# The mLSTM layer's work placed between the units of its projections and its out-projection, in a four-stage decoder trunk on one core

## The reference, cut to what matters

```python
p = h @ w_in                      # q, k (512 each), v, o (1024 each), input and forget gates (4 each)
log_f = log_sigmoid(fg + b_f)     # b = cumsum(log_f) per head
m_t = maximum(b + m, max_s(b_t - b_s + i_s))
s_qk = (q @ k.T) * exp(dmat - m_t)          # causal
num = w_inter * (q @ C) + s_qk @ v
den = w_inter * (q @ n) + sum(s_qk)
h = num / maximum(abs(den), exp(-m_t))
C_new = decay * C + sum_s w_k[s] * k_s v_s^T     # n_new, m_new likewise
out = (head_rms(h, g_head) * sigmoid(o)) @ w_out
```

## Time and profile before

| | us |
|---|---|
| median of 3 runs | 2936.16 |
| lowest, highest | 2926.19, 2954.83 |
| the profiled execution | 2929.75 |
| its span, from the first to the last instruction | 2928.2 |
| PE busy | 2748.8 |
| DVE, ACT, POOL busy | 1316.7, 883.4, 188.5 |

### The profile page before, as it was taken

The page is one execution under the profiler, slowest core; times in us unless marked ns, Lnnn a source line. Parts: engine busy times, 40 slices in busy tenths (PEclk is TensorE's granted clock), DMA queues, the critical chain, the costliest instruction groups (busy, mean ns, idle before and its releaser), DMA issues.

```text
span 2928.2 us, 49999 instructions
## 1 busy us (share of the span) xinstructions
PE 2748.8 (94%) x21504; PEld 2635.3 (90%) x21504; DVE 1316.7 (45%) x2071; ACT 883.4 (30%) x1092; POOL 188.5 (6%) x164
## 2 busy tenths in 40 slices
PE   7999999776988999999999999999799889999998
PEld 7999999745987799999999999999796875999998
DVE  5444223315466344443344433667434563444422
ACT  4332221221323233322222222443322322333322
POOL 2000000001100010000000000001210100100000
PEclk9999999985899999999999999999888989999999
DMA  4333323103257132333233333223123382333331
GB/s 122 89 93 102 95 76 88 42 8 105 84 159 251 60 93 87 93 105 90 79 91 88 107 90 79 68 67 86 29 69 101 103 286 88 87 87 92 104 93 55
DMA packets 472038, 277.42 MB, mean 95 GB/s; under 512 B 24753, under 2 KB 460722, under 8 KB 471875
## 3 DMA queue, kind: packets, MB, share of 16 engines
q1 hardware_dynamic: 458662, 239.76, 28.6%
q0 software_dynamic: 8704, 33.56, 3.2%
q10 hardware_dynamic: 4552, 2.36, 0.3%
HBM read 258.16 MB, written 17.68 MB: 94 GB/s over the span
## 4 chain that ended last, share of the span: by engine, by line
PE 86%; DVE 6%; ACT 4%; issue 2%; DMA 1%; POOL 0%; ACTq 0%; SPq 0%; DVEq 0%; POOLq 0%
PE ACC L433 24%; PE ACC L435 23%; PE ACC L434 23%; PE ACC L1119 2%; PE M L1942 1%; ACT w_hi L516 1%; PE ACC L1942 1%; PE M L1419 1%; DVE w_lo L522 1%; PE M L1462 1%; DVE cache L1215 1%; PE M L2019 1%; PE M L2081 1%; PE M L1872 0%; PE ACC L1450 0%
## 5 line engine op out<-in xcount | busy, mean ns | idle before, releaser
L433 PE MATMUL ACC<-xg_hi,w_hi 128*128 128x260 f32 x3968 | 1127.6, 284 | 11.1 <-DVE w_lo L894 7.6
L435 PE MATMUL ACC<-xg_hi,w_lo 128*128 128x260 f32 x3968 | 1123.9, 283 | 0.0
L434 PE MATMUL ACC<-xg_lo,w_hi 128*128 128x260 f32 x3968 | 1120.2, 282 | 0.0
L522 DVE TENSOR_TENSOR w_lo<-raw,w_hi 128x1024 fp32r<-128x1024 f32 (+1 forms) x330 | 426.7, 1293 | 1024.2 <-ACT w_hi L516 1019.2
L433 PEld LDWEIGHTS ACC<-xg_hi,w_hi 128*128 128x128 f32 x3968 | 750.0, 189 | 11.7 <-issue 7.7
L435 PEld LDWEIGHTS ACC<-xg_hi,w_lo 128*128 128x128 f32 x3968 | 749.2, 189 | 0.0
L434 PEld LDWEIGHTS ACC<-xg_lo,w_hi 128*128 128x128 f32 x3968 | 749.1, 189 | 0.0
L516 ACT ACTIVATE w_hi<-raw 128x1024 fp32r<-128x1024 f32 (+1 forms) x330 | 367.9, 1115 | 1207.0 <-PE ACC L435 1207.0
L434 PE MATMUL ACC<-hid_lo,w_hi 128*128 128x260 f32 x1408 | 398.3, 283 | 0.0
L435 PE MATMUL ACC<-hid_hi,w_lo 128*128 128x260 f32 x1408 | 397.6, 282 | 0.0
L433 PE MATMUL ACC<-hid_hi,w_hi 128*128 128x260 f32 x1408 | 397.4, 282 | 0.0
(11 more groups left out here) (541 smaller groups left out, 3334.1 us busy)
## 6 DMA issues: line engine op xcount, KB each, us to landing
raw<-in_ffn_w_gate SPq DMA_DIRECT2D x88, 512.0 KB, 3.8
raw<-in_ffn_w_up SPq DMA_DIRECT2D x88, 512.0 KB, 3.8
raw<-in_ffn_w_down SPq DMA_DIRECT2D x64, 704.0 KB, 4.6
cache<-in_cache_mem_k POOLq DMA_DIRECT2D x16, 1024.0 KB, 7.5
cache<-in_cache_mem_v POOLq DMA_DIRECT2D x16, 1024.0 KB, 7.4
raw<-in_gd_w_in SPq DMA_DIRECT2D x32, 512.0 KB, 4.1
raw<-in_ml_w_in SPq DMA_DIRECT2D x24, 512.0 KB, 3.9
raw<-in_xa_w_q SPq DMA_DIRECT2D x16, 512.0 KB, 3.8
```

What stands on the lines that cost most here:

```text
L433: pe.matmul(out, wh, hi[:, k0 + k, m], start=begin, stop=False)
L434: pe.matmul(out, wh, lo[:, k0 + k, m], start=False, stop=False)
L435: mm = pe.matmul(out, wl, hi[:, k0 + k, m], start=False, stop=end)
L522: dve.tensor_tensor(w_lo[:, j % 2, 0:n], raw[:, (j + d) % 4, 0:n], w_hi[:, j % 2, 0:n].bitcast(F32), ALU.subtract).then_inc(w_split, 1)
```

## The change

`ML_IN` becomes three phases of 8 units (`ML_QK`, `ML_V`, `ML_O`) with hooks, and `ML_OUT` gets hooks too. What the stage between them did is dealt out to the hooks. The hooks, where `(x, h)` is head h and `c`, `b` count value tiles and token blocks:

```diff
-            pe_phase(pe, ML_IN)
+            qk, v, g = MLX.pe_hooks(pe)
+            pe_phase(pe, ML_QK, mid=qk)
+            pe_phase(pe, ML_V, mid=v)
+            pe_phase(pe, ML_O, mid=g)
             MLX.pe(pe)
-            pe_phase(pe, ML_OUT)
+            pe_phase(pe, ML_OUT, mid=MLX.pe_updates(pe))
...
+                v = {c + 1: lambda c=c: value_rows(c) for c in (1,)}
+                v[1] = lambda: (value_rows(0), key_rows(0), key_rows(1))
+                v[3] = lambda: (value_rows(2), key_rows(2), key_rows(3))
+                v[4] = lambda: (value_rows(3), ml_dve.wait(pe, "kw", 3), self.state_query(pe, 1, 0))
+                v[5] = lambda: (value_rows(4), self.state_query(pe, 2, 16), sample_norm())
+                v[6] = lambda: (value_rows(5), state(0, 1, 0), sample_keys())
+                v[7] = lambda: (value_rows(6), state(1, 2, 1), norm_row())
+                q = {0: lambda: (value_rows(7), scores(0)), 1: lambda: (outputs(0), state(2, 4, 2))}
+                for h in range(1, MLH):
+                    q[2 * h] = lambda h=h: (self.squares(pe, h - 1), scores(h))
+                    q[2 * h + 1] = lambda h=h: (outputs(h), self.spread(pe, h - 1))
+                return {2: lambda: ml_pe.done(pe_gates(pe, 0), "gates"), 7: small_rows}, v, q
...
             def pe(self, pe):
+                self.state_query(pe, 0, 16)
+                self.squares(pe, MLH - 1)
+                ml_dve.wait(pe, "cp", MLH - 1)
+                    mm = pe.transpose(M[0:NS, c // 4, (c % 4) * P:(c % 4 + 1) * P], pm[:, 8 + c, LP:T], ident[:])
+                ml_dve.wait(pe, "n", MLH - 2)
+                self.spread(pe, MLH - 1)
+                self.state_query(pe, 3, 32)
                 ml_dve.wait(pe, "sq8")
                 ml_pe.done(pe.matmul(M[:, 3, 64:128], ones[:], ml_t8[:, 8, :], start=True, stop=True), "nsq8")
+                ml_pool.wait(pe, "yl", MLH - 2)
+                ml_dve.wait(pe, "yl", MLH - 1)
...
+                qk = {0: lambda: (act_gates(act, gm_hi, 0), self.c_load(act, 1)), 3: gate_logs, 6: gate_exps, 7: maxima}
+                v = {c + 1: lambda c=c: values(c) for c in range(7)}
+                v[0] = weights_keys
+                v[5] = lambda: (values(4), weights(0))
+                v[7] = lambda: (values(6), states(0), norm_row())
+                q = {0: lambda: values(7), 1: lambda: (squares(0), states(1), weights(1)),
+                     2: lambda: (store_states(), load_first(), self.gate(act, 0)), 3: lambda: (squares(1), weights(2)),
+                     4: lambda: self.gate(act, 1), 5: lambda: (squares(2), weights(3)),
+                     6: lambda: (self.gate(act, 2), self.high(act, 0)), 7: lambda: (load_last(), squares(3), self.high(act, 1))}
...
+                qk = {0: lambda: dve_gates(dve, gm_hi, gm_lo, 0), 2: raw_rows, 4: rows_one, 5: rows_two, 7: columns}
+                v = {1: lambda: (keys(0), keys(1)), 3: lambda: (keys(2), keys(3), masked(0)), 4: sample_norm, 5: sample_norm_two,
+                     6: sample_keys}
+                q = {0: lambda: (probs(0), masked(1)), 1: lambda: copied(0),
+                     2: lambda: (self.means(dve, own, 0), probs(1), masked(2)), 3: lambda: (copied(1), self.normed(dve, 0)),
+                     4: lambda: (self.means(dve, own, 1), probs(2), masked(3)), 5: lambda: (copied(2), self.normed(dve, 1)),
+                     6: lambda: (self.means(dve, own, 2), probs(3)), 7: lambda: (copied(3), self.normed(dve, 2))}
...
+            def pe_updates(self, pe):
+                def outer(n):
+                    h, q = ML_UPD[n // 2], n % 2
+                    if n >= 2:
+                        ml_dve.wait(pe, "C", ML_UPD[n // 2 - 1], q)
+                    for k in range(2):
+                        mm = pe.matmul(M[:, 2 * q + k, :], self.k8[:, h * P:(h + 1) * P],
+                                       ml_Ud[:, (n // 2) % 2, b:b + 2, :].rearrange("k b e -> k (b e)"), start=True, stop=True)
...
+                return {n: lambda n=n: outer(n) for n in range(8)}
...
+                roots(0)
+                gated(0)
+                roots(1)
+                gated(1)
+                low(0)
+                roots(2)
+                gated(2)
+                low(1)
+                roots(3)
+                low(2)
```

More of the change, by code:

```diff
@@ L248, in program @@
         FF10 = ffn(1, 0, "g_mix:0")
-        ML_IN = phase("ml_in", "proj", 24, KC, by4(cols_src(a["ml_w_in"][0])), norm=n_norm[0], n0=0)
+        ML_QK, ML_V, ML_O = [phase(name, "proj", 8, KC, by4(cols_src(a["ml_w_in"][0][:, at * P:(at + 8) * P])),
+                                   norm=n_norm[0] if at == 0 else None, n0=at)
+                             for name, at in (("ml_qk", 0), ("ml_v", 8), ("ml_o", 16))]
         n_norm[0] += 1
@@ L1278, in dve_attn @@
             lo(XH - 1)
[L1281 to L1295, removed]
@@ L1526, in act, with diagonal @@
-                act.wait_ge(ml_out, 16 * 5)
-            def dve(self, dve, own):
+                self.high(act, MLH - 1)
+                ml_dve.wait(act, "yl", MLH - 1)
+                ml_pool.wait(act, "yl", MLH - 2)
+                self.diagonal(act, 0)
+                act.wait_ge(ml_out, 16 * 2)
+            def diagonal(self, act, n):
+                h = ML_UPD[n]
+                if n == 0:
+                    ml_act.wait(act, "v8")
+                if n >= 2:
+                    ml_pe.wait(act, "out", ML_UPD[n - 2], 1)
+                for b in range(NS):
+                    ins = act.activation(ml_Ud[:, n % 2, b, :], ml_v8t[:, h * 256:(h + 1) * 256], ACT.Copy, scale=two[0:NS, b:b + 1])
+                ml_act.done(ins, "Ud", n)
@@ L2709, in _ @@
             sp_phase(sp, FF10[1])
-            sp_phase(sp, ML_IN)
-            sp_phase(sp, ML_OUT, others=False)
-            MLX.sp(sp)
-            sp_phase(sp, ML_OUT, first=False)
+            for ph in (ML_QK, ML_V, ML_O):
+                sp_phase(sp, ph)
+            sp_phase(sp, ML_OUT)
             GDX.sp_early(sp)
             sp_attention(sp, 0, XA0)
+            sp.wait_ge(ml_cout[1], 16)
             for ph in FF20 + FF11:
@@ L2763, in _ @@
                 act_phase(act, ph)
-            act_phase(act, ML_IN)
+            qk, v, g = MLX.act_hooks(act, own)
+            act_phase(act, ML_QK, after=qk)
+            act_phase(act, ML_V, after=v)
+            act_phase(act, ML_O, after=g)
             MLX.act(act, own)
-            act_phase(act, ML_OUT)
+            act_phase(act, ML_OUT, after=MLX.act_out(act))
+            for h in ML_UPD[0:3]:
+                act.wait_ge(ml_cout[h], 16)
             act_attention(act, own, 0, XA0)
@@ L2788, in _ @@
                 dve_phase(dve, own, ph)
-            dve_phase(dve, own, ML_IN)
+            qk, v, g = MLX.dve_hooks(dve, own)
+            dve_phase(dve, own, ML_QK, after=qk)
+            dve_phase(dve, own, ML_V, after=v)
+            dve_phase(dve, own, ML_O, after=g)
             MLX.dve(dve, own)
-            dve_phase(dve, own, ML_OUT)
+            dve_phase(dve, own, ML_OUT, after=MLX.dve_updates(dve))
+            for h in ML_UPD[0:3]:
+                dve.wait_ge(ml_cout[h], 16)
             dve_attention(dve, own, 0, XA0)
```

714 lines of the change are left out of this document (390 added, 324 removed), and 11 rows, old and new, of tables (ml_act, ml_dve, ml_pe).

## The result

The changed kernel takes 2869.98 us (median of 4 runs, 2866.95 to 2873.72) against 2938.81 of the kernel before on the same chip (4 runs, 2926.19 to 2954.83): ratio 0.9769, 95% interval 0.974 to 0.9798. I had said 2869, and faster. The profiled execution's span is 2871.0 where it was 2928.2, 57.2 less.

A forecast was written before the change was run, and what follows sets the result against it. PE alone bounds the projections; in the 204.0 us mLSTM stage engines wait for each other. Removing it and adding 143.1 (work, breaks, stalls, clock, tail, ML_OUT) gains 60.9: 2929.75 falls to 2869 us, range 2844 to 2898.

The forecast's parts named there:

- removed: The mLSTM stage between ML_IN's last unit and ML_OUT's start goes altogether: 204.0 us.
- PE's work in the hooks, full clock: PE's work added to the 24 projection units, priced per matmul from the chain: 77.0 us.
- 17 breaks: Cost of breaking into projection units, 0.36 a break from the second mixer's out-projection: 6.1 us, bounds 0 and 12.
- stalls: PE's hooks in ML_V and ML_O wait for ACT's and DVE's step: 9.3 us, bounds 4 and 15.
- clock: Lower granted PE clock, 1.7 us taken three times for the 2.4 us stalls: 5.1 us, bounds 0 and 29.
- tail: Chain of PE, DVE, POOL and ACT between ML_O's end (T) and ML_OUT's start: 28.6 us, bounds 20 and 35.
- ML_OUT: Two 512-column matmuls added in each of eight ML_OUT units, 2.12 each: 17.0 us, bounds 14 and 20.
- gain in the region: From the input projections' first unit matmul to the attention behind ML_OUT: 204.0 removed less 143.1 added, 60.9 us.
- Rival E: Moved ACT and DVE work delays the split two units ahead, PE waits in each unit: slower, 2962 us; chance 0.04.
- I take the row: For the projections' breaks, the 0.36 each measured in the second mixer's out-projection, giving 6.1 us between bounds 0 and 12.
- rival B: One-column hooks and stalls bring 1.2 GHz into many units: 29 us for 5.1, 2893 us; chance 0.18.
- Rival D: All six POOL instructions collide with DVE ahead of something PE waits for: 15 us, 2884 us; chance 0.08.

The follow-up runs named there:

- e3: Changed kernel with ML_O's hooks ahead of the last eighth of each unit's matmuls, not the last three eighths: 2858.1 us, ratio 0.9727.
- e12: The changed kernel itself run once more, without any edit: 2872.06 us, ratio 0.9799.
- e2: Changed kernel with the state updates issued one after another ahead of ML_OUT, not between its units: 2880.6 us, ratio 0.9804.
- e9: Changed kernel with all projection hooks behind ML_O and all updates ahead of ML_OUT, nothing between units: 2917.4 us, ratio 0.9949.
- e4: Changed kernel with DVE doing probs ahead of the previous head's means, PE waiting for means only ahead of the row sums: 2870.4 us, ratio 0.9769.
- e11: Changed kernel with ML_O's hooks at the last eighth, POOL's roots(3) ahead of low(1), and ML_OUT started earlier: 2861.3 us, ratio 0.9747.
- e8: Changed kernel with ML_O's hooks at the last eighth, probs before means, roots(3) before low(1), head 3's query before its spread: 2860.0 us, ratio 0.9724.
- e5: Changed kernel with POOL taking head 3's roots ahead of head 1's low half in the tail: 2866.0 us, ratio 0.9743.
- e6: Changed kernel with PE doing head 3's query ahead of the spread of head 3's roots in the tail: 2871.4 us, ratio 0.976.
- e7: Changed kernel with the one-column queries of heads 1 and 2 done twice in their hooks: 2882.5 us, ratio 0.9794.
- e10: Changed kernel with heads 1 and 2's queries as 256-column matmuls, their results left out of the outputs: 2862.5 us, ratio 0.9753.

## Why the prediction was right, point by point

The time was right to 1 us, and that is partly luck: I took the gain of 60.9 from a profiled execution (2929.75) that lies under the median before. Between the medians the gain was 68.8, between the profiled executions (2929.75 and 2872.99) 56.8. The terms, taken from starts of instructions in the profile of the changed kernel:

| term | predicted | measured |
|---|---|---|
| removed | 204.0 | 204.0 |
| PE's work in the hooks, full clock | 77.0 | 73.9 |
| 17 breaks | 6.1 | 2.4 |
| stalls | 9.3 | 7.7 |
| clock | 5.1 | 12.7 |
| tail | 28.6 | 28.6 |
| ML_OUT | 17.0 | 16.3 |
| gain in the region | 60.9 | 62.6 |

The measured column adds up to a gain of 62.4. Outside the region the profiled executions differ by 5.4 the other way: 1.3 ahead of it, 2.8 and 1.5 in the two attentions, −0.1 in the rest. In e3 and e12 the first three together are 2.1 and 2.6 shorter again, so about half of it can be scatter. The rest stays open: the first attention took 242.7 before and 244.0 to 248.1 in all thirteen profiles since, among them e2 and e9, and nothing was tried on it.

- **The bound and the plan of the sum** held: PE is busy 97% in the projections, ACT's and DVE's moved work cost nothing beyond the waits named, no unit waited for its split. Rival E didn't happen. What my sum never separated is what e9 shows: a third of the gain would have come without any placing.
- **Work**: 3 too high, mostly the small rows, 1.6 for 2.8, and scores, 2.15 each between starts for 2.35.
- **Breaks**: the step that failed is "I take the row". The 0.36 stood around 512-column matmuls of 8 rows, and there, in ML_OUT, it held (periods of 7.85). In the 24 units it is 0.14: their own matmuls took 146.4 between starts against 138.1 before, and 5.9 of the 8.3 are the clock's, which leaves 2.4 for 17 breaks.
- **Stalls**: where and in what order as said. `means` cost 0.9 and not 1.2, so heads 1 to 3 waited 1.9 for 2.4; e4 measured its share, 1.91 − 1.02.
- **Clock**: the term that was mis-sized, by 7.6. "I take that three times for the 2.4 us stalls" was right in kind: four pieces of 1.7, 6.8 in all. But that they come of the stalls is only part of it: three of four went with the stalls in e3, two in e11, and e8 kept one without any stall. What was missing is the other 5.9, the queries of heads 1 and 2, counted at 3.4 each and costing 6.9 and 6.3 with what the unit behind lost. I had the row for it, a clock of 0.50 from 694 to 740, and kept it for rival B's bound. So B was there to a third of its size (7.6 of the 24 more), hidden by 8.4 that I had too much in work, breaks and stalls.
- **Tail**: 28.6 both times. PE's part I had wrong, in two ways that cancel: I had PE through its first three pieces at T+6.1 with 6 us idle behind; the query and the squares ran at half the clock in part, to T+9.9, with 2.4 idle. The chain through DVE and POOL, which set the end, was right within 0.2: the spread at T+12.3 for 12.5. e5 and e6 show that it was the chain.
- **Rival D**: one of the six collisions fell on what PE waits for, in the tail, 2.3; e3 had two there (L1764 1.20, L1765 2.27), in a tail of 28.4.
- **ML_OUT**: right, 0.7 too high; e2 shows that the same products by themselves, with their first wait, cost nearly twice as much (36.7 − 5.6 = 31.1).

## What to carry to other kernels

Price a hook not by its duration at the full clock alone: a run of one-column matmuls costs the unit behind it too (e7), and the same product with the wide operand moving kept the clock (e10). Idle time of 0.4 to 1.9 us ahead of hooks went with more pieces at half the clock than hooks without it had. Put hooks late in the unit, so that the other engines' step, which starts at the unit's end, has time. When a stage is both rewritten and moved, build each alone, and compare in the stretch that the edit touches: profiled executions differed by 8 us in a stage that nobody had edited.

## What the runs showed of the hardware that I had not expected

- Back-to-back one-column float32 matmuls, PE busy all through, bring the granted clock from 1.00 to 0.5: 3.63 us for 16 at the full clock, 6.98 for the second pass of e7, and in the changed kernel and e7 the unit behind at 7.9 to 8.3 for 6.0. 8 matmuls of 256 columns with the same work keep 1.00.
- Among short stalls the length hardly mattered: with stalls of up to 1.9 us in ML_O (the changed kernel, e12) there were four and three pieces at half the clock, 1.7 us each, with stalls of up to 1.02 (e4) three, with stalls of 0.48 one (e3) or two (e11), and with none (e8) still one and the start of another. Where the pieces fall differs between executions of one kernel.
- The same code took 474.6 or 482.5 us in one stage in the profiles of different kernels, with DVE and ACT alike and PE at a lower clock.
- A DVE instruction of 128x4 took 1.99 us beside a POOL instruction of 128x1024, and in e3 two in a row took 1.20 and 2.27.
